# Earlier token loads, sums of squares along rows, and query and key lengths in two groups in a one-core decoder step

## The reference

```python
def rms_norm(x, g, eps=1e-6):
    xf = x.astype(jnp.float32)
    y = xf * lax.rsqrt(jnp.mean(xf * xf, axis=-1, keepdims=True) + eps)
    return (y * g.astype(jnp.float32)).astype(x.dtype)
...
def l2_normalize(x, eps=1e-6):
    return x * lax.rsqrt(jnp.sum(x * x, axis=-1, keepdims=True) + eps)
...
def mixer(h, gdn_buf, s0, conf_buf, w_in, gdn_conv_w, ...):
    proj = h @ w_in
    qkv, z, a, b, glu, gates = jnp.split(proj, SPLITS, axis=-1)
    qkv, gdn_buf_new = causal_dwconv(qkv, gdn_buf, gdn_conv_w)
    qkv = jax.nn.silu(qkv).astype(f32)
    q, k, v = jnp.split(qkv, (QK_W, 2 * QK_W), axis=-1)
    q = l2_normalize(q.reshape(bsz, t_len, GDN_HEADS, GDN_DK)) * (GDN_DK ** -0.5)
    k = l2_normalize(k.reshape(bsz, t_len, GDN_HEADS, GDN_DK))
    ...
    o, s_new = gated_delta_chunked(q, k, v, g, beta, s0.astype(f32))
...
    def block(x, mk, mv, gbuf, s, cbuf, l):
        h = rms_norm(x, norm_mix[l])
        y, gbuf, s, cbuf = mixer(h, gbuf, s, cbuf, w_in[l], ...)
        x = x + y
        x = x + cross_attn(rms_norm(x, norm_xa[l]), mk, mv, xa_q[l], xa_o[l])
        x = x + moe(rms_norm(x, norm_ffn[l]), router_w[l], router_b[l], ...)
```

## Time and profile before

| | |
|---|---|
| median of 3 runs | 1897.12 us (1894.86 to 1907.26) |
| profiled execution | 1895.7 us |
| its span, first to last instruction | 1894.0 us |
| busy: PE, DVE, ACT, POOL | 89%, 39%, 19%, 7% |
| mean granted TensorE clock | 0.948 |
| DMA over the span | 265 GB/s |

### The profile page before, as it was taken

How to read it: one execution, slowest core, us unless ns; L and a number is a source line. 1 busy time by engine, 2 the same in 40 slices (tenths; PEclk the granted TensorE clock), 3 DMA queues, 4 the chain that set the end, 5 groups by cost and what they waited for, 6 DMA issues and landing times.

```text
span 1894.0 us, 26814 instructions
## 1 busy us (share of the span) xinstructions
PE 1691.2 (89%) x9731; PEld 962.5 (51%) x9732; DVE 731.9 (39%) x1760; ACT 363.6 (19%) x991; POOL 132.9 (7%) x164
## 2 busy tenths in 40 slices
PE   5998998899999998894899999999898989889995
PEld 3765887688877576663333333333333333333332
DVE  2555587777543311506232222222322222232223
ACT  1332435545232001301000101101101010110102
POOL 2000122112211000006000000000000000000000
PEclk8996999999999998995799999999999999999997
DMA  7773655463233532581599999999999999999992
GB/s 164 153 126 56 67 106 97 76 102 108 85 111 134 169 134 90 198 314 39 218 417 416 419 416 419 416 418 418 416 419 416 419 416 418 418 417 419 417 417 116
DMA packets 146217, 501.81 MB, mean 265 GB/s; under 512 B 10641, under 2 KB 72498, under 8 KB 113216
## 3 DMA queue, kind: packets, MB, share of 16 engines
q1 hardware_dynamic: 138432, 482.37, 70.4%
q0 software_dynamic: 2704, 9.70, 1.7%
q10 hardware_dynamic: 5011, 8.79, 1.5%
HBM read 492.25 MB, written 9.43 MB: 265 GB/s over the span
## 4 chain that ended last, share of the span: by engine, by line
PE 23%; DMA 12%; SPq 10%; DVE 4%; issue 1%; ACT 1%; DVEq 0%
DMA ring<-in_moe_w 12%; PE bank L1046 11%; PE bank L1062 8%; SPq L1189 6%; SPq L1192 5%; DVE arena L1782 1%; DVE arena L1780 1%; DVE arena L1778 1%; DVE arena L1779 1%; PE bank L1053 1%; PE bank L1087 1%; ACT arena L2271 1%; PE bank L1088 1%; PE bank L1038 0%; PE bank L1019 0%
## 5 line engine op out<-in xcount | busy, mean ns | idle before, releaser
L1046 PE MATMUL bank<-ring,arena 128*64 128x512 f32 x2048 | 473.1, 599 | 14.8 <-DMA ring<-in_moe_w 11.3
L1046 PEld LDWEIGHTS bank<-ring,arena 128*64 128x64 f32 x2048 | 138.4, 137 | 291.6 <-issue 214.6
L1062 PE MATMUL bank<-ring,arena 128*64 128x512 f32 x1024 | 249.5, 644 | 24.3 <-ACT arena L2271 24.3
L1827 DVE TENSOR_TENSOR xT<-xT,bank 128x288 f32<-128x288 f32 x256 | 98.9, 448 | 294.7 <-PE bank L1088 294.7
L603 PE MATMUL bank<-hT,ring 128*128 128x288 f32 x640 | 171.2, 410 | 1.4 <-ACT arena L2027 1.4
L1062 PEld LDWEIGHTS bank<-ring,arena 128*64 128x64 f32 x1024 | 78.2, 147 | 175.1 <-issue 172.2
L544 PE MATMUL bank<-hT,ring 128*128 128x288 f32 x512 | 136.1, 426 | 13.8 <-DVE hT L1331 13.8
L1823 DVE SCALAR_TENSOR_TENSOR arena<-bank,arena 128x512 bf16<-128x512 f32 x32 | 24.0, 750 | 294.3 <-ACT arena L2257 294.3
L603 PEld LDWEIGHTS bank<-hT,ring 128*128 128x128 f32 x640 | 116.5, 192 | 27.5 <-issue 1.7
L2263 ACT ACTIVATE arena<-arena 128x512 f32<-128x512 f32 x32 | 20.2, 630 | 573.8 <-DVE arena L1778 573.8
L544 PEld LDWEIGHTS bank<-hT,ring 128*128 128x128 f32 x512 | 100.2, 199 | 48.8 <-DVE hT L1331 14.3
(11 more groups left out here) (359 smaller groups left out, 1921.8 us busy)
## 6 DMA issues: line engine op xcount, KB each, us to landing
ring<-in_moe_w SPq DMA_DIRECT2D x384, 1024.0 KB, 20.9
ring<-in_w_in SPq DMA_DIRECT2D x32, 1024.0 KB, 10.4
ring<-in_xa_kv SPq DMA_DIRECT2D x8, 1024.0 KB, 5.5
ring<-in_cache_mem_k SPq DMA_DIRECT2D x8, 1024.0 KB, 4.9
ring<-in_cache_mem_v SPq DMA_DIRECT2D x8, 1024.0 KB, 5.0
ring<-in_state_gdn POOLq DMA_DIRECT2D x8, 512.0 KB, 6.0
out_state_s<-ring POOLq DMA_DIRECT2D x8, 512.0 KB, 4.2
ring<-in_conf_pw SPq DMA_DIRECT2D x4, 1024.0 KB, 5.1
```

What stands on the lines that cost most here:

```text
L1046: last = mm(half_of(1 + q // 2, q % 2), x[:, k, :], ring[:, w_slot(k), 512 * q:512 * (q + 1)], start=False, stop=(k == KC - 1), skip_group ...
L1062: last = mm(half_of(b, n), act_T[:, f % 4, CAP * (f // 4):CAP * (f // 4 + 1)], ring[:, w_slot(KC + i), o:o + 512], start=(f == 0), stop=(f ...
L1827: tt(xT[:, c, :], xT[:, c, :], bank[SCATTER[c % 4]][:, 0:T], ALU.add).then_inc(scat_add, 1)
```

## The change

**Tokens.** The two prompt groups are loaded by two DMAs at the head of SyncE's queue, ahead of the weight pieces; the sample group and the first norm's gain stand first on ScalarE's queue. The turning of the gain alone (8 rows) joins the first group of transposes; the other vectors and the history are turned after projection job 0.

**First norm.** ScalarE squares the three groups of token rows where they landed, 1024 features in a row, with the sum of each row as a second output. VectorE and ScalarE make the inverse root of these 3 columns. VectorE multiplies the identity by each, and three products with `ones` spread the inverse over the partitions in bank 7, which VectorE reads for `hT`. Job 0 (`project_first`) waits for each chunk of `hT` by itself.

**Lengths.** Queries and keys get rows of their own (partitions 0 to 7 and 32 to 39) with an inverse each, the queries' at c = 12 to 14 of VectorE's loop, the keys' at c = 20 to 22. The spreads of the queries stand one behind each of the jobs 15 to 22, all in bank 4, and VectorE's multiplications one at the end of each step c = 16 to 23. The keys' first spread stands ahead of `head_rows(0)`, the seven others behind `head_scores(0)`, between portions of side work, and their multiplications between the steps that make the first head's matrices.

The diff, cut to its core:

```diff
-                in_jobs.append(("x", [(st_x[0:r, t, P * (4 * half + i):P * (4 * half + i + 1)], r) for i in range(4)],
+                in_jobs.append((f"x{t}", [(st_x[0:r, t, P * (4 * half + i):P * (4 * half + i + 1)], r) for i in range(4)],
                                 xT[:, 4 * half:4 * half + 4, P * t:P * t + r], (4, r)))
-        PAR_ROWS = [73, 96, 124, 124]
-        for i, r in enumerate(PAR_ROWS):
-            in_jobs.append(("par", [(st_par[0:r, i, :], r)], prm[:, P * i:P * i + r], None))
+        in_jobs.append(("gain", [(st_par[0:KC, 0, :], KC)], prm[:, 0:KC], None))
+        N_FIRST = len(in_jobs)
+        in_jobs.append(("par", [(st_par[0:73, 0, :], 73)], prm[:, 0:73], None))
+        in_jobs.append(("par", [(st_par[0:96, 1, :], 96)], prm[:, P:P + 96], None))
+        in_jobs.append(("par", [(st_par[0:124, 2 + i, :], 124) for i in range(2)],
+                        prm[:, 2 * P:4 * P].rearrange("p (i n) -> p i n", i=2)[:, :, 0:124], (2, 124)))
...
+            def project_first(n):
+
+                for k in range(KC):
+                    pe.wait_ge(*((mix_made, k + 1) if k < KC - 1 else (norm_made, 1)))
+                    last = mm(proj_bank(0), dense(n)[:, k, 0:P], hT[:, k, :], start=(k == 0), stop=(k == KC - 1))
+                last.then_inc(proj_done, 1)
...
+            def turn_in(n0, n1):
+
+                seen_load = set()
+                for kind, srcs, dst, shape in in_jobs[n0:n1]:
+                    if kind not in seen_load:
+                        pe.wait_ge(*loads[kind])
+                        seen_load.add(kind)
+                    turn(srcs)
+
+            turn_in(0, N_FIRST)
+            pe.wait_ge(diag_made, 1)
+            for t in range(TT):
+                r = TROWS[t]
+                last = mm(bank[7][:, P * t:P * t + r], ones[0:r, :], inv_diag[0:r, t, 0:r], start=True, stop=True)
+            last.then_inc(inv_spread, 1)
...
+            def l2_spread(n, sel, rows, b, read):
+
+                if read is not None:
+                    pe.wait_ge(l2_read, read)
+                mm(bank[b][:, 0:T], sel[rows], SC[rows, 2, :], start=True, stop=True).then_inc(l2_done, 1)
...
                     j = J_QKV + 2 * p_ + half
-                    project_half(j, NP["qkv", p_], half, lambda k: hT[:, k, :])
+                    if j == 0:
+                        project_first(NP["qkv", 0])
+                        turn_in(N_FIRST, N_IN_JOBS)
+                    else:
+                        project_half(j, NP["qkv", p_], half, lambda k: hT[:, k, :])
                     if 4 <= j < 4 + 2 * H:
                         if j == 4:
                             pe.wait_ge(tr_free[1], N_IN_JOBS // 2)
-                        l2_sum(j - 4, 2 * H, 5)
+                        l2_sum(j - 4, Q_ROWS if j < 4 + H else K_ROWS, 5)
+                    if 15 <= j < 15 + H:
+                        if j == 15:
+                            pe.wait_ge(gc_read, 1)
+                            pe.wait_ge(l2_inv, 1)
+                        l2_spread(j - 15, row_sel[:, j - 15, :], Q_ROWS, 4, j - 15)
...
-            def l2_spread(n, n0, count=2 * H):
-
-                if n >= 2:
-                    pe.wait_ge(l2_read, n0 + n - 1)
-                mm(bank[4 + n % 2][:, 0:T], row_sel[0:count, n, :], SC[0:count, 2, :],
-                   start=True, stop=True).then_inc(l2_done, 1)
-
-            pe.wait_ge(gc_read, 1)
-            pe.wait_ge(l2_inv, 1)
-            for n in range(2 * H):
-                l2_spread(n, 0)
-                if n % 4 == 3:
-                    fill(SIDE)
-            pe.wait_ge(banks_clear, 1)
-
...
+            pe.wait_ge(l2_inv, 2)
+            l2_spread(H, row_sel[:, H, :], K_ROWS, 4, H)
+            pe.wait_ge(banks_clear, 1)
             head_rows(0)
+            pe.wait_ge(l2_read, H + 1)
             head_scores(0)
+            for n in range(H + 1, 2 * H):
+                l2_spread(n, row_sel[:, n, :], K_ROWS, 4 + n % 2, n - 1 if n > H + 1 else None)
+                if n % 2 == 0:
+                    fill(SIDE)
             fill(SIDE)
+            fill(SIDE)
+            pe.wait_ge(l2_read, 2 * H)
...
+            sp.dma_start(st_x[:, 0, :], d["x_prompt"][0, 0:P]).then_inc(ld_x0, 16)
+            sp.dma_start(st_x[:, 1, :], d["x_prompt"][0, P:SEQ]).then_inc(ld_x1, 16)
...
-            for n, (kind, srcs, dst, shape) in enumerate(in_jobs):
-                read_bank(n, dst, shape, P, sum(r for _, r in srcs))
-            rms("norm_mix")
+            def read_in(n0, n1):
+
+                for n in range(n0, n1):
+                    kind, srcs, dst, shape = in_jobs[n]
+                    read_bank(n, dst, shape, P, sum(r for _, r in srcs))
+
+            own(V.memset(mean_sq, 1.0), mean_clear)
+            read_in(0, N_FIRST)
+            dve.wait_ge(rows_squared, TT)
+            own(ts(mean_sq, mean_sq, 1.0 / D, 1e-6, ALU.mult, ALU.add), root_in)
+            root[0] += 1
+            dve.wait_ge(root_made, root[0])
+            own(V.reciprocal(mean_sq, mean_sq))
+            for t in range(TT):
+                own(ts(inv_diag[:, t, :], ident[:, :], mean_sq[:, t:t + 1], None, ALU.mult), diag_made if t == TT - 1 else dve_self,
+                    wait=False)
+            dve.wait_ge(inv_spread, 1)
+            norm[0] += 1
+            for k in range(KC):
+                ins = stt(hT[:, k, :], xT[:, k, :], vec("norm_mix", k), bank[7][:, 0:T], ALU.mult, ALU.mult)
+                if k == KC - 1:
+                    own(ins, norm_made, norm[0])
+                else:
+                    own(ins, mix_made, wait=False)
+            read_in(N_FIRST, N_IN_JOBS)
...
-                           f, None, ALU.mult))
+                own(ts(sel[rows], ident[rows, rows].unsqueeze(2).to_broadcast((H, H, P)), factor, None, ALU.mult))
                 dve.wait_ge(sq_used, sq[0])
-                ts(SC[0:count, 2, :], bank[b][0:count, 0:T], scale, eps, ALU.mult, ALU.add).then_inc(root_in, 1)
-
-            def l2_end(count):
+                ts(SC[rows, 2, :], bank[b][rows, 0:T], scale, eps, ALU.mult, ALU.add).then_inc(root_in, 1)
+
+            def l2_end(rows):
 
                 dve.wait_ge(root_made, root[0])
-                own(V.reciprocal(SC[0:count, 2, :], SC[0:count, 2, :]), l2_inv)
+                own(V.reciprocal(SC[rows, 2, :], SC[rows, 2, :]), l2_inv)
+
+            def l2_scale(n, b):
+
+                dve.wait_ge(l2_done, n + 1)
+                own(tt(qkv[:, n, 0:T], qkv[:, n, 0:T], bank[b][:, 0:T], ALU.mult), l2_read, wait=False)
...
+                if c == 12:
+                    l2_begin(Q_ROWS, 5, 1.0, 1e-6, row_sel[:, 0:H, :], P ** -0.5)
+                if c == 14:
+                    l2_end(Q_ROWS)
+                if 16 <= c:
+                    l2_scale(c - 16, 4)
                 if c == 20:
-                    l2_begin(2 * H, 5, 1.0, 1e-6, ((slice(0, H), P ** -0.5), (slice(H, 2 * H), 1.0)))
+                    l2_begin(K_ROWS, 5, 1.0, 1e-6, row_sel[:, H:2 * H, :], 1.0)
                 if c == 22:
-                    l2_end(2 * H)
+                    l2_end(K_ROWS)
             swish(QC - 1)
...
-            for n in range(2 * H):
-                dve.wait_ge(l2_done, n + 1)
-                own(tt(qkv[:, n, 0:T], qkv[:, n, 0:T], bank[4 + n % 2][:, 0:T], ALU.mult), l2_read, wait=False)
-                if n % 4 == 3:
-                    fill()
+            l2_scale(H, 4)
...
             decay_start(0)
+            l2_scale(H + 1, 5)
+            l2_scale(H + 2, 4)
+            fill()
             key_products(0)
+            l2_scale(H + 3, 5)
+            l2_scale(H + 4, 4)
+            fill()
             inverse_start(0)
+            l2_scale(H + 5, 5)
+            l2_scale(H + 6, 4)
+            fill()
+            l2_scale(H + 7, 5)
+            fill()
             fill()
...
-            act.wait_ge(tr_free[0], 3)
-            act.wait_ge(tr_free[1], 3)
-            squares(lambda k: xT[:, k, :])
-            take_root()
+            act.wait_ge(mean_clear, 1)
+            for t, here in ((0, ld_x0), (1, ld_x1), (2, ld_x2)):
+                r = TROWS[t]
+                act.wait_ge(here, 16)
+                own(A(row_sq[0:r, :], st_x[0:r, t, :], ACT.Square, accum_out=mean_sq[0:r, t:t + 1]), rows_squared)
+            root[0] += 1
+            act.wait_ge(root_in, root[0])
+            A(mean_sq, mean_sq, ACT.Sqrt).then_inc(root_made, 1)
...
@@ -1992,8 +2073,10 @@
                 if c == 14:
                     act.wait_ge(gc_read, 1)
                     own(A(tmp_a, gc, ACT.Exp), ab_act)
+                if c == 13:
+                    l2_take_root(Q_ROWS)
                 if c == 21:
-                    l2_take_root(2 * H)
+                    l2_take_root(K_ROWS)
...
-            for _ in range(4):
-                fill()
-
             def decay(h):
 
                 act.wait_ge(decay_in, h + 1)
@@ -2146,7 +2226,8 @@
 
             key_scores(0)
             decay(0)
-            fill()
```

(6 more changed lines are left out.)

64 lines of the change are left out of this document (31 added, 33 removed).

## The result

The changed kernel takes 1928.56 us (median of 4 runs, 1923.30 to 1930.63) against 1901.32 (4 runs, 1894.86 to 1907.26): 27.2 us more, a ratio of 1.014 with a 95% interval of 1.0095 to 1.0185. The profiled execution took 1928.84, with a span of 1927.0; the one of before had 1894.0, so between the two profiles the difference is 33. Forecast were 1910 and a range to 1922, so the kernel is slower, and by more than the range allowed.

What follows compares the result with a forecast made beforehand. The expert weights' DMA stream at 416 to 419 GB/s was taken to end at a fixed distance from the front's work. -16 + 31 + 11 - 11.6 = +14.4 on 1895.7 gave 1910 us, range 1896 to 1922.

Steps and rivals of the forecast that it cites:

- The start gains 16 us: Front of the kernel: job 1 starts at 27.0 us against 42.9, 16 us gained, bounds 12 and 18.
- The jobs lose 31 us: Jobs 15 to 23: each next query spread waits for VectorE's multiplication, 8.65 us a job, 31 us lost by waits alone.
- the clock 11: Seven jobs behind those waits run partly at 1.2 GHz: 1.6 us each, 11 us lost, bounds 0 and 18.
- Job 4 of the kernel before: Row taken as model for jobs behind waits: granted clock 0.71, 5.68 us, against job 5's 4.07 at 1.00.
- From job 23 to the first head: Stage behind the last job: first head starts 25 us after job 23 against 36.6, gain 11.6, bounds 7 and 14.
- The base: Starting point of the sum: the profiled execution's 1895.7 us, 1.4 under the median of three runs.
- The faster one: Second rival: wait for VectorE doesn't bind, only eight spreads of 0.6 us are added; 1873 us, chance 0.06.
- The holding clock: First rival: the clock holds through the jobs' waits, so the 11 us drop out; 1899 us, chance 0.17.
- The jobs wholly at 1.2 GHz: Third rival: the clock never recovers between the jobs' waits, adding 17 us; 1927 us, chance 0.13.
- what the front of the program gains or loses reaches the end in full: Whole kernel: the expert stream ends at a fixed distance from the work ahead, so early shifts carry through entirely.

Runs made afterwards that it cites:

- The start alone: The kernel before with only the changed start (tokens first, squares along the rows, job 0 chunk by chunk), lengths as before: 1892.28 us, ratio 0.9943.
- the profile with the loads on SyncE: The changed kernel with ScalarE's six late loads moved to SyncE's queue, ahead of the first piece for the side work: 1924.72 us.
- at step 11: The changed kernel with ScalarE's six late loads issued behind its step 11 instead of step 0: 1931.09 us.

## Why the prediction was wrong

**The start gains 16 us.** This is the step that failed, as a term of the sum: it measured 9.8, below its lower end of 12. Up to job 1 the total holds, 27.42 against the forecast 27.0, a gain of 15.5, but partly by luck: job 0 came 2.1 us later than put (19.26 against 17.2), and job 0 with the turning behind it took 8.2 us instead of 9.8. (The steps as listed add up to 16.7 for job 0's start, not to 17.2; and sixteen loads, not fifteen, stand in ScalarE's queue before, which changes none of its times.) The sum carried the gain to the end, and only 9.8 reached job 15's sum (106.56; before 130.33 less three times 4.67, 116.3); in four other profiles with this start it was 8.0 to 11.5. 5.7 us were given back at job 4, 3.9 as the wait for the first square and 1.4 in job 5 behind it, which ran at 0.74 (5.46 us instead of 4.07), because ScalarE's late loads, which stand behind job 0's copies, were never costed: an early start moves them to where the weight pieces fill the DMA. The start alone gave 9.3 in the medians, and in the profile with the loads on SyncE 5.5 of the loss were gone. A second point is smaller: the squares begin where ScalarE's issues end, and that is not fixed at 7.7 but lay between 8.77 and 12.01 in the profiles; a square took 1.06 as estimated, plus 0.18 for an instruction that reads the sum out.

**The jobs lose 31 us, and the clock 11.** Right, mechanism and size: 78.97 - 35.1 = 43.9 against 42. A period was 10.40 against 8.65 + 1.6 = 10.25, TensorE's idle time 3.3 to 4.2 against some 3.5. Taking the wait away returned it (41.6 us for the stage), and filling it returned the clock's share (1.7 us a job against 1.6). Job 4 of the kernel before was a fair likeness: there, too, the clock was low for a part of the job only (0.51 from 58.65 to 62.00).

**From job 23 to the first head.** The direction is right, the size isn't: a gain of 7.8 (36.56 to 28.77), inside the bounds of 7 to 14, against 11.6. The clock stood at 0.64 there, and the spreads and portions of side work took from 197.05 to 214.06, 17 us instead of 14.9. They began 1 us later than put, 0.7 of it because the four groups of products for the first head took 5.1 us (191.94 to 197.05) instead of 4.4. Four other profiles with this tail took 27 to 31 us for it, at 0.69 to 0.56, so none came down to 25.

**The base.** The sum was made on an execution of 1895.7; the median of before is now 1901.3, and 1898.3 to 1901.6 in the later sets. This alone is 5.6 of the 18.6 us between 1910 and 1928.6. With 6.2 less from the start (16 against 9.8), 1.9 in the jobs and 3.8 in the tail it is 17.5; 1.1 is left, within the spread of the runs. Between the two profiles (33.0 instead of 14.4) the base drops out: the three terms make 11.9, and the second head, 6.8 longer in the profile after, makes up the rest.

**The rivals.** The faster one was excluded for the right reason, as the wait binds. The holding clock was refuted by the 0.70. The jobs wholly at 1.2 GHz gave 1927, close to what was measured, but they weren't: the mean over the stage was 0.85, and both levels stand in every period. The words "what the front of the program gains or loses reaches the end in full" are too strong: with the late state taken off, the ends of the eleven other profiles lie up to 4.7 us later against the kernel before than their first heads do.

## What to carry to other kernels

A product that frees a buffer should stand ahead of the wait for the next job, not behind that job's own work: moving one line by a step turned a loss of 27 us into a gain of 16. When a stage is made to start earlier, cost every transfer that is issued behind it on a compute engine's queue at the traffic of its new moment, or issue it from an engine that nobody waits for. Where short waits alternate with products on TensorE, count the clock as a second price of the wait, here 1.7 us beside some 4.

## What the runs showed of the hardware

Products added into waits made a kernel faster: 56 of them, with 28.7 us of TensorE's time, and yet 7.6 us less in the jobs, since the granted clock stayed at 1.00. Behind an empty wait of 3.6 us the clock fell not in the wait but 1.0 us into the job behind it. The issue of a load of 16 KB took between 3.24 and 11.33 us of the issuing engine (7.96 at step 11, 5.31 on SyncE), with the DMA full each time (share 0.98 to 1.03), so the share alone doesn't set it. ScalarE's square with a sum is two instructions, 1.06 and 0.18 us for 1024 elements.
